# Expert rows weighted and gated inside the steps and added by the scatter to residual rows in memory, with other expert pairs and the last step's rows added by products

## The reference

```python
p_grp = softmax(x @ wg + bg)                    # 4 groups
g_sel = argmax(p_grp)                           # one group per token
p_sel = p_grp[g_sel]
fine_sel = (x @ we + be) of the 8 experts of g_sel
top_v, top_i = top_k(fine_sel, 2)               # two experts of that group
w_fine = softmax(top_v) * p_sel
y = sum over the two experts of w * (silu(x @ w_gate[e]) * (x @ w_up[e])) @ w_down[e]
x = x + g2 * y                                  # g2: one gate row for latent, one for context tokens
```

## Time and profile before

| | us |
|---|---|
| median of 3 runs | 719.07 |
| the three runs | 719.07, 719.15, 717.14 |
| the profiled execution | 720.41 |
| its span, first to last instruction | 718.6 |
| TensorE busy | 581.9 (81%) |
| DVE busy | 308.8 (43%) |
| ACT busy | 186.0 (26%) |
| GpSimd busy | 126.0 (18%) |
| mean granted TensorE clock | 0.908 of full speed |

### The profile page before, as it was taken

The page is one execution under the profiler, slowest core; times in us unless marked ns, Lnnn a source line. Parts: engine busy times, 40 slices in busy tenths (PEclk is TensorE's granted clock), DMA queues, the critical chain, the costliest instruction groups (busy, mean ns, idle before and its releaser), DMA issues.

```text
span 718.6 us, 9016 instructions
## 1 busy us (share of the span) xinstructions
PE 581.9 (81%) x3187; PEld 328.4 (46%) x3188; DVE 308.8 (43%) x610; ACT 186.0 (26%) x370; POOL 126.0 (18%) x148
## 2 busy tenths in 40 slices
PE   2589988898992899989999317999999998696800
PEld 0234544455561666634555314555555554343400
DVE  3354589834566777732333471122121212021148
ACT  3100577721111677720001101111121211010121
POOL 4000214513335000000000001212122221120215
PEclk9979999999996799989999556999999999898955
DMA  7999333370000860046112371999999999999174
GB/s 303 338 374 384 153 118 118 133 305 36 0 1 8 251 269 0 2 177 251 71 58 88 141 327 34 416 420 418 423 419 417 421 418 424 420 422 397 76 278 176
DMA packets 40881, 170.34 MB, mean 237 GB/s; under 512 B 10740, under 2 KB 15816, under 8 KB 25496
## 3 DMA queue, kind: packets, MB, share of 16 engines
q1 hardware_dynamic: 30480, 152.95, 53.7%
q0 software_dynamic: 5536, 10.63, 3.9%
q10 hardware_dynamic: 4840, 6.43, 2.5%
HBM read 161.94 MB, written 17.49 MB: 250 GB/s over the span
## 4 chain that ended last, share of the span: by engine, by line
PE 64%; DVE 11%; DMA 9%; SPq 8%; ACT 3%; issue 2%; POOL 2%; POOLq 0%; DVEq 0%; ACTq 0%
PE ps L1273 14%; PE ps L1108 10%; PE ps L1207 10%; PE ps L1288 6%; SPq L216 5%; PE ps L1126 4%; DMA expert_w<-exp_w_up 4%; PE ps L1163 4%; PE ps L1190 3%; DMA w_mod_ring<-w_mod 3%; PE ps L1172 3%; SPq L219 2%; PE ps L1065 2%; PE ps L1257 2%; PE ps L1091 2%
## 5 line engine op out<-in xcount | busy, mean ns | idle before, releaser
L1273 PE MATMUL ps<-expert_w,hT_mixT 128*64 128x256 f32 x1152 | 140.8, 402 | 18.2 <-DMA expert_w<-exp_w_up 17.3
L1273 PEld LDWEIGHTS ps<-expert_w,hT_mixT 128*64 128x64 f32 x1152 | 86.2, 140 | 77.5 <-DMA expert_w<-exp_w_up 19.0
L1108 PE MATMUL ps<-hT_mixT,w 128*128 128x512 f32 (+1 forms) x256 | 73.6, 446 | 1.6 <-DVE hT_mixT L710 1.6
L1207 PE MATMUL ps<-w,hT_mixT 128*128 128x512 f32 x160 | 72.8, 612 | 0.0
L1017 DVE SCALAR_TENSOR_TENSOR w<-w,ps 128x128 f32<-128x128 f32 x36 | 10.4, 288 | 137.5 <-ACT w L529 137.5
L1288 PE MATMUL ps<-expert_w,w 128*64 128x512 f32 x288 | 65.8, 598 | 0.0
L1108 PEld LDWEIGHTS ps<-hT_mixT,w 128*128 128x128 f32 x256 | 40.2, 195 | 36.7 <-issue 35.2
L1126 PE MATMUL ps<-w_qkv,hT_mixT 128*128 128x512 f32 (+1 forms) x160 | 53.3, 491 | 0.0
L1207 PEld LDWEIGHTS ps<-w,hT_mixT 128*128 128x128 f32 x160 | 30.9, 197 | 36.7 <-issue 36.7
L529 ACT ACTIVATE w<-ps 128x128 f32<-128x128 f32 x36 | 10.0, 278 | 139.7 <-PE ps L1273 139.7
L1065 PE MATMUL ps<-w_mod_ring,silu_c 128*32 128x512 f32 x192 | 25.5, 633 | 18.7 <-DMA w_mod_ring<-w_mod 18.6
(11 more groups left out here) (206 smaller groups left out, 743.1 us busy)
## 6 DMA issues: line engine op xcount, KB each, us to landing
expert_w<-exp_w_gate SPq DMA_DIRECT2D x32, 1024.0 KB
expert_w<-exp_w_up SPq DMA_DIRECT2D x32, 1024.0 KB
expert_w<-exp_w_down SPq DMA_DIRECT2D x32, 1024.0 KB
w_mod_ring<-w_mod SPq DMA_DIRECT2D x24, 1024.0 KB, 6.4
h_rows<-h_tok ACTq DMA_DIRECT2D x10, 512.0 KB, 3.6
expert_w<-y_rows SPq DMA_DIRECT2D x10, 512.0 KB, 7.6
w<-w_in SPq DMA_DIRECT2D x4, 1024.0 KB, 11.7
w<-w_out SPq DMA_DIRECT2D x4, 1024.0 KB, 8.0
```

What stands on the lines that cost most here:

```text
L1108: ins = pe.matmul(ps[:, bank, 0:n], w1v[:, c, m * P:(m + 1) * P], HM[:, c, lo:lo + n], start=(c == 0), stop=(c == DC - 1))
L1207: ins = pe.matmul(ps[:, 2 * (t % 2) + half, :], HM[:, c, t * P:(t + 1) * P], w1v[:, c, half * 512:(half + 1) * 512], start=(c == 0), stop= ...
L1273: ins = pe.matmul(ps[r, 2 + k, 0:2 * P].rearrange("p (k f) -> p k f", k=2), xT[:, c, r], w[:, :, c, k:FF:FC], start=(c == 0), stop=(c == D ...
```

## The change

- The weight of each slot is found by a second product like that for `pid` (f32, L1247's form, into another bank), halved and used in place of the constant 0.5 in L1020. g2 is applied when the down product is evicted: `row_facts(n)` takes the step's columns (weight, is it a context row, token number) and makes `gsel`, a gate row for each slot, from g2; `y_evict(n)` multiplies all 1024 columns by it on DVE. ACT evicts nothing.
- The scatter adds (`compute_op=ALU.add`) to `out_rows`, which ACT fills beforehand with X. Empty slots go to 128 spare rows of it. `h2_rows` is written once.
- Two slots of one scatter must not name the same row. Pairs are therefore made of experts of different groups (`EXPERT`): (0, 8), (1, 9), ..., (7, 15), (16, 24), ..., (23, 31).
- The refills are written out with constant addresses instead of a loop.
- The last step isn't scattered. `out_rows` is loaded once the last scatter but one of the steps has landed, and the last step's y is added to it by products with `chosen`, a 0/1 matrix (slot by token), from PSUM.

```diff
+EXPERT = tuple(h * 2 * EPG + b * EPG + j for h in range(2) for j in range(EPG) for b in range(2))
...
+            sp.wait_ge(S["idx_mm"], 1)
+            sp.dma_start(iota, a["k_tok"].partition_broadcast(P)).then_inc(S["iota_in"], 16)
 
             def refill(q, s):
 
-                done = sp.value_load(last[0:1, bass.ds(q - HELD, 1)])
+                done = sp.value_load(last[0:1, q - HELD:q - HELD + 1])
                 sp.wait_ge(S["gu_mm"], done * FC)
-                for j in (2 * s, 2 * s + 1):
-                    w_gate_up(sp, q * 2 + (j - 2 * s), j)
+                for b in range(2):
+                    w_gate_up(sp, EXPERT[2 * q + b], 2 * s + b)
                 sp.wait_ge(S["dn_mm"], done)
...
-            refill(HELD, 0)
-            with sp.Fori(0, BODIES - 1) as it:
-                for s in (1, 2, 0):
-                    refill(it * HELD + (HELD + (s or HELD)), s)
+            for q in range(HELD, PAIRS):
+                refill(q, q % HELD)
 
             steps = sp.value_load(last[0:1, PAIRS - 1:PAIRS])
-            sp.wait_ge(S["y_out"], 16 * (steps + 1))
+            sp.wait_ge(S["y_out"], 16 * steps)
             sp.sem_inc(S["sp_turn"], 1)
             for t in range(NT):
-                for k in range(2):
-                    lo = k * TOK + t * P
-                    sp.dma_start(yk[:, k, t, :], a["y_rows"][lo:lo + P, :]).then_inc(yk_in[t], 16)
+                sp.dma_start(fin[:, t, :], a["out_rows"][t * P:(t + 1) * P, :]).then_inc(fin_in[t], 16)
...
-                for k in range(TOP):
-                    lo = k * TOK + t * P
-                    act.dma_start(a["h2_rows"][lo:lo + P, :], h2t[:, t % 2, :]).then_inc(S["h2_out"], 16)
+                act.dma_start(a["h2_rows"][t * P:(t + 1) * P, :], h2t[:, t % 2, :]).then_inc(S["h2_out"], 16)
+                act.dma_start(a["out_rows"][t * P:(t + 1) * P, :], X[:, t, :]).then_inc(S["acc_in"], 16)
...
+            act.wait_ge(S["slot"], TOP)
+            act.activation(slot1f, slot1, ACT.Copy).then_inc(S["slotf"], 1)
+            act.wait_ge(S["route_ok"], 4)
...
-                act.wait_ge(S["dn_mm"], n + 1)
-                act.wait_ge(S["y_out"], 16 * (n + 1))
-                act.activation(y[:, 512:D], ps[:, 6, :], ACT.Copy).then_inc(S["y_a"], 1)
...
-                pool.indirect_dma_start(a["y_rows"], bass.IndirectOffsetOnAxis(pidc[:, 0:1], 0), y,
-                                        None, bounds_check=TOP * TOK - 1, oob_is_err=False).then_inc(S["y_out"], 16)
+                pool.indirect_dma_start(a["out_rows"], bass.IndirectOffsetOnAxis(pidc[:, 0:1], 0), y,
+                                        None, compute_op=ALU.add).then_inc(S["y_out"], 16)
...
+            dve.tensor_tensor(step1w, hit, wts[:, :, :].rearrange("p k t -> p (k t)").unsqueeze(2)
+                              .broadcast_to([P, TOP * NT, COLS]), ALU.mult).then_inc(S["stepw"], 1)
             dve.wait_ge(S["idx_mm"], 1)
...
+            dve.wait_ge(S["route_ok"], 4)
+            step(dve.tensor_copy(info[:, :, 2], pid[:, :]))
+            step(dve.tensor_scalar(kind, info[:, :, 2], float(TOK), col["row"], ALU.is_ge, ALU.mult))
+            dve.tensor_tensor(srow[:, :], info[:, :, 2], kind, ALU.add).then_inc(S["srow"], 1)
+            step(dve.tensor_scalar(info[:, :, 1], info[:, :, 2], float(LAT), None, ALU.is_ge))
+            dve.wait_ge(S["g2_in"], 32)
+            step(dve.tensor_tensor(g2[:, 1, :], g2[:, 1, :], g2[:, 0, :], ALU.subtract))
+            dve.wait_ge(S["w_mm"], 1)
+            step(dve.tensor_scalar(info[:, :, 0], ps[:, 5, 0:COLS], 0.5, None, ALU.mult))
...
-                dve.scalar_tensor_tensor(out=act2[:, c, :], in0=sg[:, c, :], scalar=0.5, in1=ps[:, 2 + c, P:2 * P],
+                dve.scalar_tensor_tensor(out=act2[:, c, :], in0=sg[:, c, :], scalar=now[:, 0:1], in1=ps[:, 2 + c, P:2 * P],
                                          op0=ALU.mult, op1=ALU.mult).then_inc(S["act_ok"], 1)
 
+            def row_facts(n):
+
+                dve.tensor_copy(now, info[:, bass.ds(n, 1), :].rearrange("p o k -> p (o k)")).then_inc(S["now"], 1)
+                dve.wait_ge(S["now"], n + 1)
+                dve.scalar_tensor_tensor(out=gsel, in0=g2[:, 1, :], scalar=now[:, 1:2], in1=g2[:, 0, :],
+                                         op0=ALU.mult, op1=ALU.add).then_inc(S["gsel"], 1)
+
+            def y_evict(n):
+
+                dve.wait_ge(S["dn_mm"], n + 1)
+                dve.wait_ge(S["y_out"], 16 * (n + 1))
+                dve.wait_ge(S["gsel"], n + 1)
+                dve.tensor_tensor(y, wide[:, 5 * 512:5 * 512 + D], gsel, ALU.mult).then_inc(S["y_v"], 1)
+
             def step_of(n):
+                row_facts(n)
                 gated(n, 0)
                 gated(n, 1)
                 x_out(n + 1)
-                dve.wait_ge(S["dn_mm"], n + 1)
-                dve.wait_ge(S["y_out"], 16 * (n + 1))
-                dve.tensor_copy(y[:, 0:512], ps[:, 5, :]).then_inc(S["y_v"], 1)
+                y_evict(n)
...
+            def finish(t):
+
+                b = 2 * t % 8
+                dve.wait_ge(fin_in[t], 16)
+                dve.wait_ge(S["tail_mm"], t + 1)
+                dve.tensor_tensor(fin[:, t, :], fin[:, t, :], wide[:, b * 512:b * 512 + D], ALU.add)\
+                   .then_inc(S["fin"], 1)
...
+            pe.wait_ge(S["slotf"], 1)
+            pe.wait_ge(S["stepw"], 1)
+            for i in range(TOP * NT):
+                ins = pe.matmul(ps[:, 5, 0:COLS], slot1f[:, i, :], step1w[:, i, :],
+                                start=(i == 0), stop=(i == TOP * NT - 1))
+            ins.then_inc(S["w_mm"], 1)
...
+            for t in range(NT):
+                if t >= 4:
+                    pe.wait_ge(S["fin"], t - 3)
+                for half in range(2):
+                    ins = pe.matmul(ps[:, 2 * t % 8 + half, :], chosen[:, t * P:(t + 1) * P],
+                                    y[:, half * 512:(half + 1) * 512], start=True, stop=True)
+                ins.then_inc(S["tail_mm"], 1)
```

More of the change, by code:

```diff
@@ L58 @@
 N_SMALL = 120
-TABLE = (("rev", NE), ("pairno", TOP * NT), ("full", BLOCKS - 1), ("count", PAIRS), ("half", NE), ("edge", COLS + 1),
+TABLE = (("rev", NE), ("revg", NG), ("row", 1), ("pairno", TOP * NT), ("full", BLOCKS - 1), ("count", PAIRS), ("half", NE), ("edge", COLS + 1),
          ("slot", P))
@@ L90, in build @@
         wts = sb("pair_weight", [P, 2, NT])
+        final = sb("final_step", [P, 1], U32)
         tab = sb("routing_table", [P, sum(n for _, n in TABLE)])
@@ L163, in build @@
         xT = hmf[:, 0:D].rearrange("p (c n) -> p c n", c=DC)
+        iota = hmf[:, D:D + TOK]
+        chosen = hmf[:, D + TOK:D + 2 * TOK]
+        step1w = hmf[:, 3400:3400 + TOP * NT * COLS].rearrange("p (k n) -> p k n", k=TOP * NT)
+        info = hmf[:, 4700:4700 + 3 * COLS].rearrange("p (n k) -> p n k", k=3)
+        now = hmf[:, 4900:4903]
+        kind = hmf[:, 4910:4910 + COLS]
+        slot1f = W1[:, 5 * D:5 * D + TOP * NT * P].rearrange("p (k n) -> p k n", k=TOP * NT)
         y = W1[:, 0:D]
+        gsel = W1[:, D:2 * D]
         xg = W1[:, 2 * D:3 * D]
@@ L187, in build @@
         wd_in = [sem(f"wd_in{i}") for i in range(HELD)]
-        yk_in = [sem(f"yk_in{i}") for i in range(NT)]
+        fin_in = [sem(f"fin_in{i}") for i in range(NT)]
         used = dict.fromkeys(("v", "p", "act"), 0)
@@ L226, in every_step, with every_step_but_last @@
             return steps
+        def every_step_but_last(e, body):
+            end = e.value_load(final[0:1, 0:1])
+            with e.Fori(0, end) as n:
+                body(n)
+            return end
         @block.sync
@@ L914, in _ @@
             step(dve.tensor_scalar(off, eqg, 1.0, BIG, ALU.subtract, ALU.mult))
-            step(dve.tensor_tensor(fine.rearrange("p t (g e) -> p t g e", g=NG),
-                                   logit[:, :, NG:].rearrange("p t (g e) -> p t g e", g=NG),
-                                   off.unsqueeze(3).broadcast_to([P, NT, NG, EPG]), ALU.add))
+            for h in range(2):
+                half = lambda v: v[:, :, h * 2 * EPG:(h + 1) * 2 * EPG].rearrange("p t (j b) -> p t j b", b=2)
+                step(dve.tensor_tensor(half(fine), half(logit[:, :, NG:]),
+                                       off[:, :, 2 * h:2 * h + 2].unsqueeze(2).broadcast_to([P, NT, EPG, 2]), ALU.add))
             best = [scratch(9, 1), scratch(10, 1)]
@@ L1314, in with_partition @@
     lo = {name: sum(n for _, n in TABLE[:i]) for i, (name, _) in enumerate(TABLE)}
-    t[:, lo["pairno"]:lo["pairno"] + TOP * NT] += np.arange(P)[:, None]
+    for name, n in (("pairno", TOP * NT), ("row", 1)):
+        t[:, lo[name]:lo[name] + n] += np.arange(P)[:, None]
     return t.astype(np.float32)
```

115 lines of the change are left out of this document (56 added, 59 removed).

## The result

The changed kernel takes 731.86 us (729.37 to 735.39, four runs) against 719.06 before: ratio 1.0188, 95% interval 1.014 to 1.0236, 12.8 us slower. The forecast was 736.9, 17.8 slower.

The account below looks back on a forecast made before the run. The prediction took the DMA stream of expert weights as the bound. Its terms, 12.2 - 1.0 + 1.3 + 0 + 27.1 - 21.8 = +17.8 us, on 719.07 gave 736.9 us; range 715 to 756, the forecast's own 730 to 744.

Parts of the forecast that it names:

- The bound: Expert stage: the DMA stream of expert weights sets the time by its start and bytes; TensorE's own work does not.
- DVE's added work: Expert steps: DVE's eviction of all 1024 columns and gate rows stay hidden, by 1 us; size 0.
- rival D: Scatter so slow that eviction waits for it every step: some 65 us above the forecast, 800 us; chance 0.08.
- Term 1: Release of the weight ring: the first pair has two steps, so the stream starts one step later, +12.2 us.
- Term 2: Start, routing to first expert step: added products delay the transposes, +1.3 us; up to 2.8 back if the clock rises sooner.
- Term 4: Scatter in the stream: 128 rows a step, each accumulating row costing two row times, +27.1 us (bounds +8.3 and +45.8).
- Term 5: Tail after the last down product: loads pass under the last step, products add its y; 14.3 instead of 36.1 us, -21.8.
- The estimate by the ratio 1.93: Scatter in the stream: a skill page's measured ratio for two source reads would make the added cost 25 us.
- A: Scatter: accumulating and spare rows take no stream time; sum -9.3 us, 709.8 us; chance 0.11.
- B: Scatter: an added row costs a plain row; sum -1.0 us, 718.1 us, or 715.3 with the clock up sooner; chance 0.19.
- C: Scatter: an added row costs three row times; sum +36.5 us, 755.6 us; chance 0.12.

Follow-up runs that it names:

- e3: The changed kernel with a bounds check on the accumulating scatter, so empty slots are skipped instead of added to 128 spare rows: 728.87 us, ratio 1.0165.
- e1: The changed kernel with pairs (16, 24) to (23, 31) first, so the doubled pairs are numbers 8 and 13 instead of 0 and 5: 723.76 us, ratio 1.0075.

## Why the prediction was right, point by point

**The bound** was right: the stream's engines are full from the first refill until the last loads, TensorE waits for exp_w_up (40.9 us in ten waits, 17.3 in five before), and everything that moved the start or the bytes of the stream moved the time. DVE's added work was hidden; eviction did wait for the scatter. Timeline of DVE in the changed kernel:

```profile
460.17 1.23 DVE L1054 TENSOR_TENSOR w<-ps,w 128x1024 f32<-128x1024 f32 x1 [3.32 <-PE ps L1331]
461.31 0.16 DVE L1044 COPY hT_mixT<-hT_mixT 128x3 f32 x1
461.50 1.28 DVE L1046 SCALAR_TENSOR_TENSOR w<-w,hT_mixT 128x1024 f32<-128x1024 f32 x1
...
473.67 1.22 DVE L1054 TENSOR_TENSOR w<-ps,w 128x1024 f32<-128x1024 f32 x1 [4.58 <-DMA out_rows<-w,slot_row_now]
```

Timeline of GpSimd, the scatter that the second of these evictions waited for:

```profile
462.21 2.06 POOL L640 DMA_INDIRECT out_rows<-w,slot_row_now  x1 [3.96 <-DVE w L1054]
...
473.92 0.18 POOL L636 COPY slot_row_now<-slot_out_row 128x1 uint32 x1 [3.66 <-DMA out_rows<-w,slot_row_now]
```

It landed within 11.7 us (forecast 11.6), and the eviction began some 1.3 us after it could have (4.58 us of waiting instead of 3.32; forecast 1.7). In the whole stream seven evictions waited for a scatter, the longest 7.1 us, and TensorE never waited for an eviction: all its ten waits are for exp_w_up. So nothing came of it, and rival D, a scatter too slow by itself, is out.

**Term 1** (release, +12.2): right. From the first gate/up product to the first refill are 10.9 us more, which is the step of 12.2 less a first product that ran 1.3 us faster. The kernel before with the doubled pair first measures +12.8 (+10 to +16 by its interval, forecast 11), and the changed kernel without it -8.1 and -9.6 (both -8 by the ratios).

**Term 2** (start, +1.3): about right, but not to be read from one pair of executions. From the second f16 product (424.79 after, 429.09 before) to the first gate/up product are 9.06 us instead of 7.92, and the added products took 4.49 us and ended just ahead of the gather. The first gate/up product then ran 8.87 us instead of 10.21, which would give the whole term back, out of the 2.8 that I had kept as a bound. It isn't the change that does this. In the ten kernels with the added products this stretch takes 8.6 to 10.2 us (mean 9.8) and the product 8.8 to 10.2 (mean 9.5); in the four without them 7.9 to 8.9 (mean 8.3) and 9.1 to 10.2 (mean 9.8). Together the term is +1.1 in the mean. The added products ran at the lower level (granted clock 0.50), and no run shows that they bring the clock up sooner.

**Term 4** (scatter, +27.1, less 1.0 for the step that fell ahead of the stream): right in kind, too large in time. The plain write shows two row times, and the engines' time in the stream (share times length) rose from 220.6 to 248.3 us, by 27.7 where 26.1 were forecast. But the stream grew by only 20.7 us, and its pairs came 18.2 us apart (571.18 to 698.48, seven pairs), not 19.1. The step that was off is the one from the engines' time to the stream's: it took the 0.99 of before as full for both. Before, some engines stood idle at the end (4 us of all of them, after 1), since skipped rows load them unevenly; with 128 rows in every scatter they are loaded nearly alike, and the share is 1.02. The same difference took half of the saving from e3. The mean number of rows underrates what a partly filled transfer costs.

**Term 5** (tail, -21.8): -21.4. The products ran 8.82 us at the full clock after a gap of 1.6 us, as forecast (8.5).

**Not in the sum:** the last gate/up product ran 9.07 us instead of 7.47, and this one is on the path: 1.6 us of this pair of executions. TensorE waits more often than before, and its granted clock in the stream is 0.92 instead of 0.97. But the last product also ran 9.07 us in the kernel before filled from both ends, which is as fast as the kernel before (1.0013), after a wait of 1.99 us, and 7.42 in e1, where it doesn't wait. So this piece isn't shown to be the change's.

**The sum** of 17.8 stands against 13.0 in the profiles and 12.8 in the medians. Of the 4.8 us between forecast and profiles, 5.4 are term 4 and 1.5 the start (a faster first product in this execution), less 1.7 for the last step and 0.4 for the tail. The last gate/up product was forecast at about 710 and began at 698.5, for the same reasons and the 4.3 us of the execution. The estimate by the ratio 1.93 was given as 25; 1.93 x 128 rows less 71, 4 KB each at 420 GB/s in 15 steps, are 26. A plain row's 8.3, the low bound, and three row times, 45.8, are both far from the 20.7.

**The rivals:** A (added reads free) and B (one row time) are refuted by the plain write, C (three) by the same run, D by TensorE's waits.

## What to carry to other kernels

When a ring of weights is refilled as work is done, and the transfer engines are the bound, the time at which the first buffer is released is the start of the bound. A piece of work of double length belongs behind the first few buffers; near the end the compute engine becomes the bound again (e1), though here that cost nothing that the times could show. The accumulating scatter counted as two transfers, rows to spare places included, and a tail of load and store was worth putting under the last step. Engine time isn't elapsed time: a saving in rows counts only as far as it falls on the fullest engine, and a share below 1 at the end of a stream, with nothing left to issue, is where to look. Reordered and with the empty rows skipped, this change is 0.5% faster than the kernel before; as made it is 1.9% slower.

## What the runs showed of the hardware

- The packets of an accumulating scatter of 128 rows of 4 KB held the DMA engines for 2.0 times as long as those of a plain one (47 against 23 us of 16 engines for 17 scatters), while bytes are counted once.
- GpSimd was busy 2.06 us with issuing the accumulating scatter of 128 rows and 1.48 with the plain one (both without a bounds check); the plain one with a bounds check took 1.03.
- An accumulating scatter with a bounds check that skips empty rows took GpSimd 2.00 us to issue (e3).
- The same rows at other partitions are not the same transfer: full slots spread in blocks of 8 partitions cost 6.5 us over some 18 gathers and 18 scatters, and the second half filled from its other end cost nothing (ratio 1.0013).
- When rows are skipped the DMA engines finish unevenly: their share in the last 16 us before the last awaited weights was 0.48 to 0.75, and 0.97 to 0.99 when all 128 rows were written. Which partitions are served by which engine isn't shown.
